# Start addresses of TensorE's operands: stationary on multiples of 128 bytes, moving 64 bytes over

## What is computed

```python
# layer 1: attention (8 heads, T5 bias) beside a linear recurrent unit, then a gated FFN
proj = rms_norm(x) @ w_in;  mix = concat([attn, lru]) @ w_out;  x = x + rms_norm(mix)
up = causal_dwconv(rms_norm(x) @ w_up);  x = x + rms_norm((gelu(c_g) * c_u) @ w_down)
# layer 2: neighborhood attention (16 heads) and a SwiGLU FFN, both modulated by c @ w_ada
x = x + g_a * (neighborhood_attention(h, w_qkv) @ w_o);  x = x + g_f * ((silu(h @ gate) * (h @ up)) @ w_down)
# layer 3: latent attention (w_down, w_uq, w_ukv, w_o) and 8 experts of width 1792, top 2
x = x + g_a * mla(h);  x = x + g_f * moe(h, w_router, w_gu, w_down)
out = rms_norm(x) * final_norm
```

## Time and profile before

| | us |
|---|---|
| median of 3 runs | 1275.49 (1274.8 to 1276.27) |
| the profiled execution | 1273.2 |
| its span (first to last instruction) | 1271.0 |
| TensorE busy / weight loads busy | 1229.8 / 1095.1 |
| VectorE / ScalarE / GpSimd busy | 1021.7 / 782.6 / 92.5 |
| mean granted clock of TensorE | 0.996 of 2.4 GHz |

### The profile page before, as it was taken

One profiled execution on the slowest core, in us unless ns is written; L12 is line 12 of the kernel. 1 busy time (PEld: TensorE's weight loads), 2 busy tenths in 40 slices (PEclk: granted clock), 3 DMA queues, 4 the chain that ended last, 5 costly groups with the idle time before them and its releaser, 6 DMA issues.

```text
span 1271.0 us, 20171 instructions
## 1 busy us (share of the span) xinstructions
PE 1229.8 (97%) x7626; PEld 1095.1 (86%) x7626; DVE 1021.7 (80%) x1099; ACT 782.6 (62%) x997; POOL 92.5 (7%) x111
## 2 busy tenths in 40 slices
PE   6989999999999999999999999999999999999995
PEld 5978999987988799998888678898989898989884
DVE  6888799986765577776847569889898989898997
ACT  5775666544555454443436656777777777777774
POOL 0020000000572100000001302000000000000020
PEclk9999999999999999999999999999999999999998
DMA  9963897678954569988984139999999999999992
GB/s 310 340 236 104 300 323 264 225 283 262 250 164 166 170 215 329 308 299 335 352 267 160 48 116 379 397 392 366 390 353 394 356 406 347 407 346 406 345 410 95
DMA packets 163839, 369.09 MB, mean 290 GB/s; under 512 B 24405, under 2 KB 96416, under 8 KB 157368
## 3 DMA queue, kind: packets, MB, share of 16 engines
q1 hardware_dynamic: 157201, 350.72, 77.3%
q10 hardware_dynamic: 5094, 12.11, 2.7%
q0 software_dynamic: 1472, 5.28, 1.1%
HBM read 360.72 MB, written 14.70 MB: 295 GB/s over the span
## 4 chain that ended last, share of the span: by engine, by line
PE 68%; DVE 13%; DMA 5%; issue 4%; ACT 4%; SPq 3%; POOL 2%; ACTq 0%; DVEq 0%
PE ps L1308 19%; PE ps L774 7%; PE ps L776 7%; PE ps L775 7%; PE ps L1335 6%; PE ps L787 3%; PE ps L789 3%; PE ps L791 3%; DVE wlo L1893 3%; SPq L690 2%; PE ps L839 2%; PE ps L847 2%; DVE alo L1893 2%; DVE wlo L1886 2%; DVE acc_ends L1987 1%
## 5 line engine op out<-in xcount | busy, mean ns | idle before, releaser
L1373 ACT ACTIVATE whi<-raw 128x1024 fp32r<-128x1024 f32 x190 | 197.0, 1057 | 165.3 <-PE ps L776 109.1
L1886 DVE TENSOR_TENSOR wlo<-raw,whi 128x1024 fp32r<-128x1024 f32 x190 | 233.9, 1258 | 79.9 <-ACT whi L1373 77.0
L774 PE MATMUL ps<-ahi,whi 128*128 128x256 f32 x864 | 247.1, 286 | 2.9 <-DVE alo L1918 2.7
L776 PE MATMUL ps<-ahi,wlo 128*128 128x256 f32 x864 | 245.2, 284 | 0.0
L775 PE MATMUL ps<-alo,whi 128*128 128x256 f32 x864 | 245.1, 284 | 0.0
L1893 DVE TENSOR_TENSOR wlo<-raw,whi 128x1792 fp32r<-128x1792 f32 (+1 forms) x96 | 199.3, 2089 | 22.7 <-ACT whi L1386 22.3
L1386 ACT ACTIVATE whi<-raw 128x1792 fp32r<-128x1792 f32 (+1 forms) x96 | 167.1, 1755 | 53.7 <-PE ps L1308 25.2
L774 PEld LDWEIGHTS ps<-ahi,whi 128*128 128x128 f32 x864 | 166.6, 193 | 4.4 <-issue 3.9
L775 PEld LDWEIGHTS ps<-alo,whi 128*128 128x128 f32 x864 | 166.5, 193 | 0.7 <-issue 0.7
L776 PEld LDWEIGHTS ps<-ahi,wlo 128*128 128x128 f32 x864 | 166.5, 193 | 0.0
L1308 PE MATMUL ps<-whi,hchi 128*128 128x448 f32 x352 | 102.6, 373 | 1.9 <-DVEq L2494 1.2
(11 more groups left out here) (351 smaller groups left out, 2399.3 us busy)
## 6 DMA issues: line engine op xcount, KB each, us to landing
raw<-in_moe_w_gu SPq DMA_DIRECT2D x96, 896.0 KB, 6.9
ada<-in_w_ada SPq DMA_DIRECT2D x48, 1024.0 KB, 7.1
raw<-in_moe_w_down SPq DMA_DIRECT2D x32, 1024.0 KB, 7.8
ada<-in_moe_w_gu SPq DMA_DIRECT2D x32, 896.0 KB, 7.2
raw<-in_w_up SPq DMA_DIRECT2D x22, 1024.0 KB, 6.2
raw<-in_ffn_w_gu SPq DMA_DIRECT2D x22, 1024.0 KB, 8.9
ada<-in_moe_w_down SPq DMA_DIRECT2D x16, 1024.0 KB, 9.0
raw<-in_na_w_qkv SPq DMA_DIRECT2D x12, 1024.0 KB, 8.5
```

Of the source, the lines that this page charges most:

```text
L774: pe.matmul(o, h[:, k, cols], bhi[:, k], start=(k == 0), stop=False)
L776: m = pe.matmul(o, l[:, k, cols], bhi[:, k], start=False, stop=(k == KT - 1))
L1373: act.activation(high_, src, ACT.Copy).then_inc(hi_done, 1)
L1886: ve.tensor_tensor(low_, src, high_.bitcast(F32), ALU.subtract).then_inc(lo_done, 1)
```

## The change

`LINE` becomes 128, and pads of 64 bytes (`room(HALF_LINE)`; 16 columns of 4 bytes) shift some buffers. By the addresses that follow, `raw`, `whi`, `wlo`, `ada`, `xn`, `mixed`, `ghi`, `glo`, `hchi`, `gchi` and their lo parts stay at 0 modulo 128; `ahi`, `alo`, `hx`, `lat_hi` and `lat_lo` come to 64; `cst` stays at 64. `hx` no longer shares `xn`'s start but begins 64 bytes ahead of it. A slot of `whi` and `wlo` grows by 128 bytes. Where weights move, the split parts are written and read 64 bytes further into slots 0 and 1 (`by_rows`, `split_of`, `split_of_expert`); in the third slot they lie at `ahi`, which is at 64 itself. Where weights are stationary, they stay at the slot's start.

With this the two operands of a matmul stand to each other as follows:

| matmuls | before: stationary, moving | after |
|---|---|---|
| columns form, latent tiles | 0, 0 | 0, 64 |
| rows form with ghi, glo, mixed; experts | 0, 0 | 0, 64 |
| rows form with ahi, alo; values (L1187) | 0, 0 | 64, 64 |
| F32 with raw and hx | 0, 0 | 0, 64 |
| sums on L943 (acc stationary, ones of cst moving) | 0, 64 | 0, 64 |

A chunk whose mate lies at the other offset now waits for both halves of it (`same`). No instruction is added, removed or moved on any engine.

```diff
-LINE = 64
+LINE = 128
+HALF_LINE = 16
 CHUNK = 2048
+SLOT = CHUNK + 2 * HALF_LINE
...
-        whi2 = at("whi", NSPLIT * CHUNK, F32R).rearrange("p (s n) -> p s n", s=NSPLIT)
-        wlo2 = at("wlo", NSPLIT * CHUNK, F32R).rearrange("p (s n) -> p s n", s=NSPLIT)
+        whi2 = at("whi", NSPLIT * SLOT, F32R).rearrange("p (s n) -> p s n", s=NSPLIT)
+        wlo2 = at("wlo", NSPLIT * SLOT, F32R).rearrange("p (s n) -> p s n", s=NSPLIT)
...
+        hx_at = room(2 * HALF_LINE) + HALF_LINE * 4
         xn_at = room(NT * D)
         xn = at("xn", NT * D, offset=xn_at).rearrange("p (t n) -> p t n", t=NT)
-        ahi_flat = at("ahi", KT * S, F32R)
+        room(HALF_LINE)
+        ahi_at = room(KT * S)
+        ahi_flat = at("ahi", KT * S, F32R, offset=ahi_at)
...
-        hx = at("hx", NT * D, offset=xn_at).rearrange("p (t k s) -> p t k s", t=NT, k=KT)
+        hx = at("hx", NT * D, offset=hx_at).rearrange("p (t k s) -> p t k s", t=NT, k=KT)
...
+        here[0] += HALF_LINE * 4
         lat_hi = u("lat_hi", 3 * S, F32R).rearrange("p (k s) -> p k s", k=3)
...
+        moved_at = [HALF_LINE, HALF_LINE, 0, 0]
+
+        def by_rows(c):
+
+            if W_QKV <= c < W_NAO:
+                return QKV_ORDER[c - W_QKV][1] == 2
+            return W_IN + 8 <= c < W_UP or W_DOWN <= c < W_QKV or W_NAO <= c < W_GU or W_DN2 <= c < W_MDN or W_MLO <= c < W_MOE
+
+        def split_of(c):
+
+            half = Chunk(c).half
+            n = moved_at[half] if by_rows(c) else 0
+            return [w[half][:, n:n + CHUNK] for w in (whi, wlo)]
+
+        def split_of_expert(ck):
+
+            n = moved_at[ck.half]
+            return [w[ck.half][:, n:n + CHUNK] for w in (whi, wlo)]
...
-                ck = Chunk(c)
-                h, l = (view(w[ck.half], k_tiles, width) for w in (whi, wlo))
+                h, l = (view(w, k_tiles, width) for w in split_of(c))
...
-                            h, l = (view(w[ck.half], 2, EH) for w in (whi, wlo))
+                            h, l = (view(w, 2, EH) for w in split_of_expert(ck))
...
-                same = ck.mate is None or chunk_shape(c) == chunk_shape(ck.mate)
+                same = ck.mate is None or (chunk_shape(c), by_rows(c)) == (chunk_shape(ck.mate), by_rows(ck.mate))
```

More of the change, by code:

```diff
@@ L521, in expert_shape, with split_values @@
             return (2, EH) if c < 16 else (1, D) if c in (16, PASS_CHUNKS - 1) else (2, D)
+        moved_at = [HALF_LINE, HALF_LINE, 0, 0]
[10 more added lines that the diff above has]
+            return [w[ck.half][:, n:n + CHUNK] for w in (whi, wlo)]
+        def split_values():
+            half = Chunk(W_UKV).half
+            n = D + moved_at[half]
+            return [w[half][:, n:n + D] for w in (whi, wlo)]
         def part_of(slot_ap, c, q):
@@ L533, in parts_of @@
             ck = Chunk(c)
-            src, split_ = raws[ck.slot], (whi[ck.half], wlo[ck.half])
+            src, split_ = raws[ck.slot], split_of(c)
             if c == W_UKV:
                 src = src.rearrange("p (h two d) -> p two h d", two=2, d=HD)[:, q]
-                return [src] + [w[:, q * D:(q + 1) * D].rearrange("p (h d) -> p h d", d=HD) for w in split_]
+                halves_ = split_values() if q else [w[:, 0:D] for w in split_]
+                return [src] + [w.rearrange("p (h d) -> p h d", d=HD) for w in halves_]
             if W_UQ <= c < W_MLO:
@@ L764, in columns_form @@
             def columns_form(c, outs, bhi, blo, turn0=None, between=None):
-                ck = Chunk(c)
-                h, l = (view(w[ck.half], KT, 256) for w in (whi, wlo))
+                h, l = (view(w, KT, 256) for w in split_of(c))
                 for f, o in enumerate(outs):
@@ L1148, in latent_tile @@
             def latent_tile(c, col, ks, o):
-                ck = Chunk(c)
-                h, l = whi[ck.half], wlo[ck.half]
+                h, l = split_of(c)
                 for n, k in enumerate(ks):
@@ L1180, in _ @@
             begin(W_UKV, 1)
-            h, l = (w[Chunk(W_UKV).half][:, D:2 * D] for w in (whi, wlo))
+            h, l = split_values()
             for t in range(NT):
@@ L1330, in expert_pass @@
                     ck = begin_expert(c, p)
-                    h, l = (view(w[ck.half], kc, D) for w in (whi, wlo))
+                    h, l = (view(w, kc, D) for w in split_of_expert(ck))
                     for k in range(kc):
@@ L1385, in split_expert @@
                 k, n = expert_shape(c)
-                act.activation(whi[ck.half][:, 0:k * n], raws[ck.slot][:, 0:k * n], ACT.Copy).then_inc(moe_hi, 1)
+                high_, _ = split_of_expert(ck)
+                act.activation(high_[:, 0:k * n], raws[ck.slot][:, 0:k * n], ACT.Copy).then_inc(moe_hi, 1)
             def square(s, t, src, n=D):
@@ L1892, in split_expert @@
                 k, n = expert_shape(c)
-                ve.tensor_tensor(wlo[ck.half][:, 0:k * n], raws[ck.slot][:, 0:k * n],
-                                 whi[ck.half][:, 0:k * n].bitcast(F32), ALU.subtract).then_inc(moe_lo, 1)
+                high_, low_ = split_of_expert(ck)
+                ve.tensor_tensor(low_[:, 0:k * n], raws[ck.slot][:, 0:k * n], high_[:, 0:k * n].bitcast(F32), ALU.subtract)\
+                    .then_inc(moe_lo, 1)
             def root(s, t):
```

## The result

| | before | after |
|---|---|---|
| median (runs) | 1275.88 us (4) | 1268.68 us (4) |
| lowest and highest | 1274.8, 1276.85 | 1267.74, 1269.44 |
| span of the profiled execution | 1271.0 us | 1267.5 us |

The ratio of the runs is 0.9943, with an interval of 0.9929 to 0.9957: 7.2 us less, where 45 were forecast. The profiled execution of after is the longest of its four (1269.44 us), and that of before, 1273.2 us, is shorter than all four above, so the two spans show 3.5 us of it.

The account below looks back on a forecast made before the run. TensorE's matmul cost, start to start, was taken as the bound. Of 61.0 us of gains 45 come through: span 1271.0 - 45 = 1226, plus 4.5 gives 1230 us; its own range 1207 to 1250, overall 1207 to 1282.

Parts of the forecast that it names:

- the second rival: F32R matmuls: the 13 ns are weight exchange or fixed cost, no address matters; 1275.5 us (1273 to 1278), chance 0.27.
- (a): F32R matmuls with stationary at 0, moving at 64: gain 10.4 ns each, 12.9 for 448 columns, together 61.0 us.
- (b): Matmuls with both operands at 64 (ahi or alo stationary): no gain counted; 5.2 us more if moving offset alone matters.
- What came through: Share of the 61.0 us reaching kernel time, with other engines close behind TensorE: 6 + 9 + 5 + 6 + 19 = 45 us.
- Other columns forms: The other 672 columns-form matmuls, in the input and QKV projections: 5 of 7.0 us come through.
- Experts: Eight expert passes: 2.6 of 3.35 us in each of six middle passes, 1.5 in first and last; 19 us.
- (d): Later ScalarE waits before splits of input and QKV chunks: costed at nothing; 5.3 us without the cover.
- (c): Plain F32 matmuls, hx moving over raw, 112 ns each: the change costs and gives nothing.
- Rival 3: Slower: 4464 shifted matmuls of 256 and 512 columns each pay 2.5 ns, 11.2 us; 1286.7 us, chance 0.16.
- Rival 1: Only part of the excess goes, as only some read phases separate: a quarter to half of 45 us; 1253 to 1264, chance 0.15.
- the signs: Profile after: columns form near 110 ns, 448 columns 190, 512 columns 216, VectorE above 95%, pass below 59 us.

Follow-up runs that it names:

- the fifth experiment: Computation left out: series of 32 F32R matmuls with a load each, stationary at 0 modulo 2048 bytes, moving operand 0 to 496 bytes further; no kernel time given.
- the seventh experiment: Changed kernel with slots 8448 bytes apart and a distance per form: columns form 64, 448 columns 64, 512 columns 0; 1267.53 us, ratio 0.9939.
- the tenth: The changed kernel itself, unaltered, profiled once more; 1270.92 us in one execution, span 1269.0 us.
- the first experiment: Changed kernel with moving weights back at their slots' start and the waits of before; ahi, alo, hx and latents stay at 64; 1267.24 us, ratio 0.9923.
- the second experiment: Changed kernel with ahi, alo, hx and the latents back at 0; moving weights stay 64 bytes further; 1279.79 us, ratio 1.0023.
- the third: Computation left out: series of 64 F32R matmuls with own loads, moving at 0 to 112 bytes, stationary at 0 or 64, other engines idle; no kernel time given.
- the eighth kernel: As the seventh experiment, but with the columns form at distance 192 instead of 64; 1261.68 us, ratio 0.9881.

## Why the prediction was wrong

The sign was right and the place too: start addresses do matter, and by the distance of the two operands, so the two reads of TensorE act on each other in some way. With that the second rival (no address matters) is refuted. The Trainium skill's sentence behind it (TensorE: Matmul & The Clock Gate, "Step-by-step: what each phase is for") says that weights and moving operand come through two independent ports, so that a load takes no bandwidth from the running matmul. For the time of F32R matmuls with a load each, this case does not agree: one kernel has 120.0 and 113.3 ns for 256 columns and 226.7 and 233.2 for 512, and only the distance differs. Whether the ports or something behind them is shared, no run shows, and no series was run without the loads: that it takes both reads is argued from the distance.

**The step that failed is the price of (a).** I took the excess of F32, 2.9 ns, as what would be left, a gain of 10.4 ns (12.9 for 448 columns). That reads the 13.3 ns as one cost that all F32R forms share and that an address removes. By the runs it is two:

- 448 and 512 columns keep at least 13.3 ns at every distance tried. What they share with 256 columns is the size of the excess, not its cause. Term by term: 19.8 us forecast for 448 columns, 1536 x 0.9 = 1.4 measured; 6.0 and 7.0 us for 512 columns, measured a loss of 480 x 4.2 + 672 x 3.4 = 4.3 us.
- 256 columns have another bound, near 112 ns for a matmul with its own load (L282 in the fifth experiment). The earlier trace rows have the number but can't tell it from a stream: L839 and L943 move 128 columns of F32, which at two cycles each are 106.7 ns. A row of the kernel before that I did not read can: 8 columns of F32 with a load each. From the second start on they stand 112 ns apart, at granted clock 1.00.

```profile
744.34 1.84 PE L1234 MATMUL ps<-rscaled,xT 128*128 128x8 f32 x16
746.04 0.68 PE L810 MATMUL ps<-cst 128*128 128x512 f32 x1
```

Had I taken 112 as the bound, (a) would have been 2592 x 8 = 21 us at most for this form, and 27.0 could not stand. Measured: 2592 x 5.5 = 14.3 us, as part of the chunks ran at 117.8. And this much was partly luck. I reckoned modulo 128, where 64 and 192 are one place, and with the new slot length slot 0 came to stand at 192 and slot 1 at 64. Where all chunks stand at 64, in the seventh experiment, 53 of 54 run at 117.8, a gain of 2.3 ns instead of 5.5.

- The sum that TensorE could give is then 14.3 + 1.4 - 4.3, and some tenths for the latents and the (b) forms: about 11 us, not 61.
- A slip in the sums beside it: the whole of 61.0 and 5.2 us off 1275.5 is 1209, not 1207.

**What came through**, which I had as 45 of 61, was closer. First gate and up projection: 6 forecast, 4.4 measured. VectorE is busy in 96% of the window shown above, and TensorE pauses ahead of five of the last six chunks (starts 0.21 to 0.31 us apart); four of the six ran at 117.8. Second: 9 forecast, 5.7 measured, which is all that its cadence gives (816 x 6.7 ns and 144 x 2.2). Other columns forms: 5 forecast; the input stage became 1.3 us shorter in this profile (in the tenth, of the same kernel, it is 0.6 us longer than before), and the QKV stage lost 2.9, 1.8 of them ahead of its first chunk. In the kernel after, TensorE waits there behind ScalarE for 1.6 us; in the first experiment, which has no later waits, an idle time of 2.1 us stands at the same place, so these 1.8 are not (d). Experts: 19 forecast, none measured in a middle pass: its 448 columns gained 0.9 ns and its 512 columns lost 3.4. From the first expert chunk to the end it is a loss of 2.3 us. That the passes would follow a faster TensorE is not refuted: with 200.2 and 226.8 a pass fell from 61.42 to 61.1.

**(b)**, both at 64, is nearly neutral in its 256 columns (119.2 against 119.8) and lost 2.4 ns in its 512 columns. By the addresses its operands stand 128 bytes apart modulo 256 in slot 0 and 0 apart in slot 1, for which the table has 118.3 and 120.0 ns, and 233.2 and 226.7. That `SLOT` moves slot 1 by 128 bytes was in the diff, and I let it pass since I reckoned modulo 128.

**(c)** was right: F32 with raw and hx takes 111.7 ns before and after. **(d)** was nearly right: against the first experiment, without the waits, the stage that differs most is QKV (136.3 us after, 135.0 there, 133.3 before), so about 1.3 us there could be theirs. In the profile after TensorE waits 1.8 us longer for GpSimd's `probs` in it than in the first experiment's; whether (d) is behind that is not shown.

**Rival 3** (slower) had the right form in the wrong place: a shift that makes matmuls of 512 columns dearer did come, 3.4 to 4.2 ns instead of 2.5. It lost to the columns form in the sum, and in the second experiment, where that gain is missing, it rules: 1.0023. Its reason does not stand: the 2.5 ns that 448 columns had extra are gone at distances 16 and 64 (200.0 ns), so they are no cost of their length. **Rival 1**, a part of the excess because some phases fall apart and some don't, with 1253 to 1264 us, was the nearest in mechanism. It too was reckoned from a full size that wasn't there. Of the signs, VectorE above 95% between 140 and 250 us came true (96%), starts near 110, 190 and 216 ns and a pass below 59 us did not.

## What to carry to other kernels

Before an excess is booked as a gain, look for a row in which the supposed cause is gone and the cost remains; here that was the 112 ns of 8 columns with their own load (L1234). Check an address argument against the stride of the slots, not their first one only. If TensorE alternates loads and F32R matmuls, try the distance of moving and stationary operand modulo 256 bytes for each width by itself: 192 for 256 columns, 64 for 448, 0 for 512 gave 14.8 us of 1276.5 here (ratio 0.9881), and with 64 for 256 columns it was 8.1 of 1275.6 (ratio 0.9939).

## What the runs showed of the hardware

- F32R matmuls with a load each cost 113.3 to 120.0 ns (256 columns), 200.0 to 206.7 (448) and 226.7 to 234.6 (512). In the fifth kernel this goes by the distance of the two operands modulo 256 bytes; in the third, 11 of 47 series are 1.4 to 6.7 ns off that. With other engines and DMA idle or busy the times are the same to 0.1 ns.
- In 448 and 512 columns 13.3 ns above columns at 2.4 GHz remain at the best distance. A matmul with its own load of 128 columns takes no less than about 112 ns at 2.4 GHz (64 columns of F32R; 8 columns of F32, L1234), and 213.3 ns at 1.2 GHz (8 and 128 columns of F32R).
- At distances 64 and 192 the 256-column form has two lasting values, 113.3 and 117.8 ns. In the eighth kernel 113.3 ran through all 20 chunks of one projection and 117.8 through all 20 of the other, with the same addresses. 448 columns at distance 0 have 202 to 203 and 206 to 207.
